# Branch weights ahead of the gate quarters in a group's loads, and the token sums of a layer in 40 GpSimd pieces

## The chip, the cores and the metric

The kernel runs on one core of a Trainium2 chip. The metric is the device time of one execution in microseconds (us), the median of several runs. Engines are named as in the profile: PE is TensorE, DVE is VectorE, ACT is ScalarE, POOL is GpSimd, SP is SyncE, whose queue (SPq) issues most DMAs here.

## The reference, cut to what matters

Two layers of an encoder with 768 tokens (512 of a prompt, 256 of a sample), width 1024. Each layer projects the normed input `h` to three token mixers (A, B, C), to their SiLU gates `z` and to their sigmoid gates `g`, merges the branches and projects once more:

```python
for i, y_i in enumerate((ya, yb, yc)):
    z = cols(COL_Z + i * BRANCH_WIDTH, BRANCH_WIDTH)
    g = cols(COL_G + i * D_MODEL, D_MODEL)
    u = jax.nn.sigmoid(g) * ((y_i * jax.nn.silu(z)) @ w_br[i])
    merged = u if merged is None else merged + u
out = merged @ w_out
return x + gate[:, None, :] * out
```

Everything is fp32. A product of fp32 precision is made of three matmuls on a high and a low part of each operand (`w_hi`, `w_lo`, `act_hi`, `act_lo`): ACT rounds the high part, DVE subtracts it for the low part.

## The kernel before

**Units.** The whole program is one list, `UNITS`. Each engine walks through this list in a loop of its own and does its share of each unit, so the program order on every engine is that of the list, and semaphores tie the engines together. A layer has, in this order: units `("q", l, kind, h, g, t)`, the projection of one tile of 128 tokens to query, key and value of one head (24 matmuls of 128x384 on PE, 6 tiles a head; mixer C has three head groups g), with the attention of earlier tiles between; units `z` for the SiLU gates (8 for each mixer, those of C last); then the gate stage, 12 groups `(l, kind, j)` of 11 units each, kinds in the order C, A, B with four groups each; then 16 output units `o`.

**A group of the gate stage.** The gate projection `h @ w_g` of a group is made by seven products in place of eight (a Strassen-like scheme on halves of the tokens and of the contraction). Units `s0` to `s6` are these products, in the order T1, W11, T2, W22, T3, W21, T4, and units `b0` to `b3` are the four blocks of the branch projection `y @ w_br`. Each of the 11 units is 12 matmuls of 128x384. The four quarters W12, W11, W22, W21 of the group's gate weights are loaded by `load_quarters`, POOL makes T1 to T4 of them (`combos`, 128x512 each), ACT and DVE split each into `s_hi` and `s_lo`. The branch weights are one load of 128x1024 (`load_branch`, into one of two buffers `wb_raw` by turns), split by `branch_high` on ACT (`wb_hi`, line 1718) and `branch_low` on DVE (`wb_lo`, line 2254).

**What runs one group ahead.** While PE works on a group, the others prepare the next one. ACT calls `branch_high` of the next group at unit `s3`, ahead of the sigmoids of `s3` to `s6`. DVE calls `branch_low` of the next group at unit `s4`, ahead of the sums of product T3 (`add_up`, lines 2233 and 2236). PE may start `s6` of the group only when the first of those sums (`U3`) is there. All three engines work strictly in their order.

**Loads of the stage.** `load_groups` on SP calls for each group `load_quarters` (but for the first group of a layer, whose quarters come earlier), then `load_branch`, then, for the first group of A and of B, `load_back`, which brings the parked output `y_t` of that mixer back. The queue waits in its order: W12 of a group for the use of `w12` by the group before (`combo_ready` of T3), W11, W22 and W21 for the group before to finish its units `s1`, `s3` and `s5`, and the branch weights for `b3` of the group two before, whose buffer they take. `back_high` on ACT and `back_low_part` on DVE split `y_t` in the units `s5` to `b0` of these two groups, and their `b0` needs the four results.

**Token sums.** The scheme also needs sums of quadrants of the activations, S1 to S4, in `mix_raw` (128 x 4 x 4 x 384). POOL makes them in `mixes(l)`: ten `tensor_tensor` instructions of 128x1536 one behind the other. They stand at unit `("q", l, "C", 0, 2, 0)` in POOL's program, but wait only for the end of `move_high` and `move_low` (`hi_moved`, `lo_moved`: the activations are put in the order of mixer C at its first unit) and, in layer 1, for the last outputs of layer 0. ACT and DVE split them (`mix_high`, `mix_low`) beside the last `z` units.

## Time and profile before

| | |
|---|---|
| median of 3 runs | 2671.23 us (2670.93 to 2673.95) |
| the profiled execution | 2670.71 us, its span 2667.1 us |
| PE busy | 2376.2 us (89%) |
| DVE busy | 1592.4 us (60%) |
| ACT busy | 1118.9 us (42%) |
| POOL busy | 251.2 us (9%), 219 instructions |
| DMA | mean 70 GB/s |
| mean granted PE clock | 0.948 of full speed |

The span is what the profiler saw between the first and the last instruction; the 3.6 us to the execution's time lie outside of it. A row of a timeline is: start, duration (both in us from the span's start), engine, line, instruction, output and inputs, sizes, count, and in brackets the idle time before it with what ended it. Ends of matmuls are modelled, so the pace of PE is read from starts. A wait is put down to the last of several releasers.

### The profile page before, as it was taken

The page shows a single profiled execution, that of the slowest core. Times are in us where ns is not written, and L with a number is a line of the kernel's source. Part 1 is how long each engine was busy: PE and PEld are TensorE (multiplying, and loading weights), DVE is VectorE, ACT ScalarE, POOL GpSimd, SP SyncE. Part 2 cuts the span into 40 slices and gives each one's busy share as a digit, 9 for nine tenths or more (in the row PEclk, how much of TensorE's full clock was granted, in tenths as well). Part 3 has the DMA queues.
Part 4 walks back from the last instruction along what each step waited for, and adds up shares of the span by engine and source line. Part 5 has one row for each costly group of instructions (what it writes and reads, how often), then busy time and mean ns, then how long its engine had stood idle before and what let it go on. Part 6 is the DMA issues. An engine that isn't in the chain of part 4 may idle for free.

```text
span 2667.1 us, 41810 instructions
## 1 busy us (share of the span) xinstructions
PE 2376.2 (89%) x15466; PEld 2195.4 (82%) x15466; DVE 1592.4 (60%) x4305; ACT 1118.9 (42%) x3035; POOL 251.2 (9%) x219
## 2 busy tenths in 40 slices
PE   7999987999999777777999999599999997777789
PEld 5788876999998777777888889499999977777788
DVE  7875678566765433343578757866667653343452
ACT  5666554344444322222446655444444342222230
POOL 0100133000000111111001002600000001111100
PEclk9999998999999888888999999899999998888899
DMA  7112210211113112121520122002111121121213
GB/s 281 69 64 70 102 56 20 87 53 51 49 64 114 43 47 70 48 69 42 161 70 31 41 94 61 26 27 105 51 53 51 74 83 49 44 76 44 75 58 120
DMA packets 63033, 186.10 MB, mean 70 GB/s; under 512 B 9584, under 2 KB 22512, under 8 KB 59888
## 3 DMA queue, kind: packets, MB, share of 16 engines
q1 hardware_dynamic: 52320, 164.00, 17.8%
q10 hardware_dynamic: 10512, 19.44, 2.1%
q8 instruction: 124, 2.03, 0.3%
q14 instruction: 77, 0.63, 0.1%
HBM read 168.73 MB, written 12.58 MB: 68 GB/s over the span
## 4 chain that ended last, share of the span: by engine, by line
PE 77%; DVE 9%; DMA 5%; ACT 5%; issue 4%; SPq 0%; DVEq 0%; ACTq 0%
PE ps_proj L1034 51%; PE ps_score L1078 7%; PE ps_pt L1078 7%; DMA wb_raw<-in_w_branch 4%; PE ps_score L1211 2%; PE ps_pt L1224 2%; PE ps_pv L1260 1%; PE ps_score L1195 1%; PE ps_tr L1275 1%; PE ps_pv L1241 1%; ACT wb_hi L1718 1%; PE ps_tr L1276 1%; DVE qk L2054 1%; PE ps_pv L1254 1%; DVE w_lo L2316 1%
## 5 line engine op out<-in xcount | busy, mean ns | idle before, releaser
L1034 PE MATMUL ps_proj<-w_hi,act_hi 128*128 128x384 f32 x1824 | 635.3, 348 | 3.3 <-ACT act_hi L1485 2.2
L1034 PE MATMUL ps_proj<-w_lo,act_hi 128*128 128x384 f32 x1824 | 614.1, 337 | 0.0
L1034 PE MATMUL ps_proj<-w_hi,act_lo 128*128 128x384 f32 x1824 | 614.1, 337 | 0.0
L1034 PEld LDWEIGHTS ps_proj<-w_hi,act_hi 128*128 128x128 f32 x1824 | 344.8, 189 | 9.1 <-ACT act_hi L1485 5.8
L1034 PEld LDWEIGHTS ps_proj<-w_lo,act_hi 128*128 128x128 f32 x1824 | 345.2, 189 | 0.0
L1034 PEld LDWEIGHTS ps_proj<-w_hi,act_lo 128*128 128x128 f32 x1824 | 344.3, 189 | 0.0
L2003 DVE TENSOR_REDUCE ssq<-square 128x2 f32<-128x256 f32 (+1 forms) x228 | 95.6, 419 | 251.2 <-ACT square L1579 250.0
L1078 PE MATMUL ps_pt<-act_hi,s_hi 128*128 128x384 f32 x96 | 51.9, 540 | 178.0 <-DVE sum L2233 178.0
L1579 ACT ACTIVATE square<-ps_proj 128x256 f32<-128x256 f32 x228 | 88.1, 386 | 281.5 <-PE ps_proj L1034 281.1
L2316 DVE TENSOR_TENSOR w_lo<-w_raw,w_hi 128x1536 fp32r<-128x1536 f32 (+3 forms) x121 | 188.5, 1559 | 14.5 <-ACT w_hi L1409 13.9
L1034 PE MATMUL ps_proj<-act_hi,w_hi 128*128 128x512 f32 (+1 forms) x512 | 176.1, 344 | 12.7 <-DVE w_lo L2316 9.3
L1409 ACT ACTIVATE w_hi<-w_raw 128x1536 fp32r<-128x1536 f32 (+2 forms) x120 | 161.0, 1342 | 59.7 <-DMA w_raw<-in_w 34.7
L1078 PEld LDWEIGHTS ps_pt<-act_hi,s_hi 128*128 128x128 f32 x96 | 29.6, 308 | 185.0 <-DVE sum L2233 185.0
L1034 PE MATMUL ps_proj<-act_lo,w_hi 128*128 128x512 f32 (+1 forms) x512 | 173.9, 340 | 0.0
L1034 PE MATMUL ps_proj<-act_hi,w_lo 128*128 128x512 f32 (+1 forms) x512 | 173.8, 339 | 0.0
L2254 DVE TENSOR_TENSOR wb_lo<-wb_raw,wb_hi 128x1024 fp32r<-128x1024 f32 x24 | 30.6, 1276 | 218.0 <-ACT wb_hi L1718 218.0
L979 POOL TENSOR_TENSOR s_raw<-w,s_raw 128x512 f32<-128x512 f32 x24 | 32.9, 1370 | 1235.8 <-DMA s_raw<-in_w_gate 1220.5
L1718 ACT ACTIVATE wb_hi<-wb_raw 128x1024 fp32r<-128x1024 f32 x24 | 25.3, 1056 | 286.7 <-DMA wb_raw<-in_w_branch 286.7
L1034 PE MATMUL ps_proj<-yz_hi,wb_hi 128*128 128x384 f32 x384 | 134.5, 350 | 3.1 <-DVE yz_lo L2264 2.8
L1034 PE MATMUL ps_proj<-yz_lo,wb_hi 128*128 128x384 f32 x384 | 132.9, 346 | 0.0
L1034 PE MATMUL ps_proj<-yz_hi,wb_lo 128*128 128x384 f32 x384 | 132.1, 344 | 0.0
L1601 ACT ACTIVATE rstd_ln<-ssq,eps 128x2 f32<-128x2 f32 (+1 forms) x240 | 71.4, 297 | 142.9 <-DVE ssq L2003 142.9
(263 smaller groups left out, 5468.0 us busy)
## 6 DMA issues: line engine op xcount, KB each, us to landing
w_raw<-in_w SPq DMA_DIRECT2D x80, 768.0 KB, 5.1
w_raw<-in_w SPq DMA_DIRECT2D x40, 512.0 KB, 3.8
s_raw<-in_w_gate SPq DMA_DIRECT2D x72, 256.0 KB, 3.3
w_ada<-in_w_mod SPq DMA_DIRECT2D x11, 1536.0 KB, 6.7
wb_raw<-in_w_branch SPq DMA_DIRECT2D x24, 512.0 KB, 4.8
first_ada<-in_w_first SPq DMA_DIRECT2D x8, 1024.0 KB, 12.8
parked<-y_t ACTq DMA_DIRECT2D x4, 1536.0 KB, 6.6
w<-in_w_gate SPq DMA_DIRECT2D x24, 256.0 KB, 4.4
```

The source lines that it names most:

```text
L979: pool.tensor_tensor(s_raw[PLACE[c]][:], first[:], second_[:], ALU.subtract).then_inc(*combo_ready.inc((g, c)))
L1034: op = pe.matmul(out, sta[s](k), mov[m](k), start=(k == 0 and n == 0), stop=(k == chunks - 1 and n == 2))
L1078: op = pe.matmul(sum_bank(u), (s_hi, s_lo)[s][i][:, k, :], moved_in(x, m)[:, k, :], start=opens and k == 0 and n == 0, stop=k == HK - 1 an ...
L1211: op = pe.matmul(ps_score[:, c0:c0 + keys], q, k, start=True, stop=True)
L1224: op = pe.transpose(crossed_probs(a)[:, n * P:(n + 1) * P], probs[ATT_AT[a] % 2][:, c0:c0 + P], ident[:])
L1409: act.activation(w_hi[b][:, c0:n], w_raw[b][:, c0:n], ACT.Copy).then_inc(*w_hi_ready.inc(p))
L1579: act.activation(square[:], made(u, 0, 256), ACT.Square).then_inc(*sq_ready.inc(u))
L1601: act.activation(rstd_ln[:, 0:segs], squares_of(u), ACT.Ln, bias=eps[:], scale=1.0 / d).then_inc(*ln_ready.inc(u))
L1718: act.activation(wb_hi[b][:], wb_raw[b][:], ACT.Copy).then_inc(*wb_hi_ready.inc(g))
L2003: dve.tensor_reduce(squares_of(u), square[:].rearrange("p (s d) -> p s d", s=segs), AX.X, ALU.add).then_inc(*ssq_ready.inc(u))
L2254: dve.tensor_tensor(wb_lo[b][:], wb_raw[b][:], wb_hi[b][:].bitcast(F32), ALU.subtract).then_inc(*wb_lo_ready.inc(g))
L2316: return dve.tensor_tensor(w_lo[b][:, c0:c1], w_raw[b][:, c0:c1], w_hi[b][:, c0:c1].bitcast(F32), ALU.subtract)
```

## The change

In `load_groups` the branch weights of a group are issued ahead of its four quarters:

```diff
             def load_groups(l):
                 for g in groups_of(l):
+                    load_branch(g)
                     if group_before(g):
                         load_quarters(g)
-                    load_branch(g)
                     if g[2] == 0 and g[1] in PARKED:
                         load_back(l, g[1])
```

`mixes(l)` becomes `mix_piece(l, n, k)`, one quarter (128x384) of one of the ten steps. The 40 pieces of a layer stand at 40 successive `q` units of mixer C, beginning with `("q", l, "C", 0, 2, 0)`, and each waits for PE to have finished the projection of its unit:

```diff
+MIX_PIECES = [(n, k) for n in range(10) for k in range(HK)]
...
+            def mix_piece(l, n, k):
...
+                if n > 0:
+                    pool.wait_ge(*mix_step.at((l, n - 1, k)))
+                elif k == 0:
+                    pool.wait_ge(*hi_moved.at((l, KC)))
+                    pool.wait_ge(*lo_moved.at((l, KC)))
...
+                pool.tensor_tensor(out, a, b, op).then_inc(*mix_step.inc((l, n, k)))
...
-                if u[0] == "q" and u[2:] == ("C", 0, 2, 0):
-                    mixes(u[1])
+                if u[0] == "q" and u[2] == "C" and AT[u] >= AT[("q", u[1], "C", 0, 2, 0)]:
+                    at = AT[u] - AT[("q", u[1], "C", 0, 2, 0)]
+                    if at < len(MIX_PIECES):
+                        pool.wait_ge(*proj_ready.at(u))
+                        mix_piece(u[1], *MIX_PIECES[at])
...
-                act.wait_ge(*mix_step.at((l, 9)))
+                act.wait_ge(*mix_step.at((l, *MIX_PIECES[-1])))
```

The number of instructions on PE, DVE, ACT and SP stays the same; POOL has 60 more. Line numbers of the changed kernel are one higher from here on.

SP's queue at the start of the gate stage of layer 0, before (`w` is W12, `s_raw_147`, `_149` and `_151` are W11, W22 and W21, `wb_raw_158` and `_159` the two branch buffers; the first row is the branch load of the layer's first group):

```order
L869 DMA wb_raw_158<-in_w_branch 128x1024 [waits proj_ready]
L860 DMA w_153<-in_w_gate 128x512 [waits combo_ready]
L860 DMA s_raw_147<-in_w_gate 128x512 [waits proj_ready]
L860 DMA s_raw_149<-in_w_gate 128x512 [waits proj_ready]
L860 DMA s_raw_151<-in_w_gate 128x512 [waits proj_ready]
L869 DMA wb_raw_159<-in_w_branch 128x1024 [waits proj_ready]
L860 DMA w_153<-in_w_gate 128x512 [waits combo_ready]
```

The same place in the changed kernel:

```order
L870 DMA wb_raw_158<-in_w_branch 128x1024 [waits proj_ready]
L870 DMA wb_raw_159<-in_w_branch 128x1024 [waits proj_ready]
L861 DMA w_153<-in_w_gate 128x512 [waits combo_ready]
L861 DMA s_raw_147<-in_w_gate 128x512 [waits proj_ready]
L861 DMA s_raw_149<-in_w_gate 128x512 [waits proj_ready]
L861 DMA s_raw_151<-in_w_gate 128x512 [waits proj_ready]
L870 DMA wb_raw_158<-in_w_branch 128x1024 [waits proj_ready]
```

The second group's branch load has moved ahead of the four quarters, and with it ahead of the queue's waits for `s1`, `s3` and `s5` of the first group.

SP's queue where kind A opens in layer 0, in the changed kernel (the parked `y_t` of A, then the next group's loads):

```order
L861 DMA s_raw_151<-in_w_gate 128x512 [waits proj_ready]
L877 DMA y_t<-parked 128x1536 [waits park_done,proj_ready]
L877 DMA y_t<-parked 128x1536
L870 DMA wb_raw_159<-in_w_branch 128x1024 [waits proj_ready]
L861 DMA w_153<-in_w_gate 128x512 [waits combo_ready]
```

The branch load of the group behind now follows the two loads of `y_t` directly, where four quarters stood between before.

POOL's program at the sums of a layer, before (ten instructions, then the first group's combination T1):

```order
L965 TENSOR_TENSOR bias_97<-rel_s,mask_b_sb 128x256 [waits masked]
L965 TENSOR_TENSOR bias_97<-rel_s,mask_b_sb 128x256
L1015 TENSOR_TENSOR mix_raw<-act_hi 128x1536 [waits lo_moved,hi_moved]
L1015 TENSOR_TENSOR mix_raw<-act_lo 128x1536 [waits mix_step]
L1015 TENSOR_TENSOR mix_raw<-mix_raw 128x1536 [waits mix_step]
L1015 TENSOR_TENSOR mix_raw<-act_hi 128x1536 [waits mix_step]
```

The same place in the changed kernel:

```order
L966 TENSOR_TENSOR bias_97<-rel_s,mask_b_sb 128x256 [waits masked]
L966 TENSOR_TENSOR bias_97<-rel_s,mask_b_sb 128x256
L1016 TENSOR_TENSOR mix_raw<-act_hi 128x384 [waits lo_moved,hi_moved,proj_ready]
L1016 TENSOR_TENSOR mix_raw<-act_hi 128x384 [waits proj_ready] x3
L1016 TENSOR_TENSOR mix_raw<-act_lo 128x384 [waits mix_step,proj_ready] x4
L1016 TENSOR_TENSOR mix_raw<-mix_raw 128x384 [waits mix_step,proj_ready] x4
L1016 TENSOR_TENSOR mix_raw<-act_hi 128x384 [waits mix_step,proj_ready] x4
```

Each instruction of before is four now, and each of them waits for a projection unit of its own (`proj_ready`).

## Rows read from the trace of the kernel before

**Rows 1.** The page: the span, and the chain that ended last, by line.

```profile
span 2667.1 us, 41810 instructions
...
PE ps_proj L1034 51%; PE ps_score L1078 7%; PE ps_pt L1078 7%; DMA wb_raw<-in_w_branch 4%; PE ps_score L1211 2%; PE ps_pt L1224 2%; PE ps_pv L1260 1%; PE ps_score L1195 1%; PE ps_tr L1275 1%; PE ps_pv L1241 1%; ACT wb_hi L1718 1%; PE ps_tr L1276 1%; DVE qk L2054 1%; PE ps_pv L1254 1%; DVE w_lo L2316 1%
```

**Rows 2.** Waits of the whole span: us in total, times, longest.

```profile
ACT wb_hi L1718 <- DMA wb_raw<-in_w_branch: 286.7, 22, 13.7
...
PE ps_pt L1078 <- DVE sum L2233: 178.0, 22, 8.9
```

**Rows 3.** Timeline of one group of kind C, layer 0, engine by engine.

```profile
960.76 8.65 SPq L860 DMA_DIRECT2D s_raw<-in_w_gate  x3
969.46 0.43 SPq L869 DMA_DIRECT2D wb_raw<-in_w_branch  x1
...
974.25 1.06 ACT L1718 ACTIVATE wb_hi<-wb_raw 128x1024 fp32r<-128x1024 f32 x1 [12.99 <-DMA wb_raw<-in_w_branch]
...
975.34 1.23 DVE L2254 TENSOR_TENSOR wb_lo<-wb_raw,wb_hi 128x1024 fp32r<-128x1024 f32 x1 [9.86 <-ACT wb_hi L1718]
...
977.09 0.69 PE L1078 MATMUL ps_pt<-act_hi,s_hi 128*128 128x384 f32 x1 [8.04 <-DVE sum L2233]
...
983.95 0.33 PE L1034 MATMUL ps_proj<-yz_hi,wb_hi 128*128 128x384 f32 x1
...
990.19 0.33 PE L1078 MATMUL ps_score<-mix_hi,s_hi 128*128 128x384 f32 x1
```

**Rows 4.** The chain in order of time: first and last branch wait of layer 0.

```profile
902.16 5.67 DMA wb_raw<-in_w_branch
...
1240.07 4.65 DMA wb_raw<-in_w_branch
```

**Rows 5.** Parked `y_t`: landing times of its DMAs; the opening of kind A.

```profile
DMA to landing us min/median/max: 4.3/5.9/7.6
...
1046.72 1.83 DVE L2264 TENSOR_TENSOR yz_lo<-y_t,yz_hi 128x768 fp32r<-128x768 f32 x2 [1.32 <-ACT yz_hi L1731]
...
1051.30 0.44 PE L1034 MATMUL ps_proj<-yz_hi,wb_hi 128*128 128x384 f32 x1 [0.32 <-DVE yz_lo L2264]
```

**Rows 6.** Windows: us, busy time of PE, PEld, DVE, ACT, POOL, granted clock, DMA.

```profile
388.80:424.50 35.70, 8.28 (x52) 7.42 (x51) 35.29 (x24) 4.17 (x16) 34.58 (x11) 0.69 0.02 4
1698.00:1734.00 36.00, 9.17 (x56) 8.07 (x52) 35.62 (x23) 4.54 (x18) 34.95 (x11) 0.66 0.02 4
...
914.00:1260.00 346.00, 263.86 (x1370) 259.20 (x1370) 131.08 (x213) 83.97 (x154) 52.01 (x41) 0.86 0.16 54
...
425.00:870.00 445.00, 442.48 (x3418) 415.71 (x3418) 288.74 (x1033) 196.93 (x564) 5.08 (x4) 0.99 0.19 66
```

**Rows 7.** The start of mixer C, layer 0: the sums on POOL, DVE, PE.

```profile
L1015 POOL TENSOR_TENSOR mix_raw<-act_hi x4: 3416/3418/3428, 388.8 to 1709.0; 128x1536 f32<-128x1536 f32 x4
...
396.14 6.81 DVE L2118 TENSOR_SCALAR probs<-probs,rden 128x256 f32<-128x256 f32 x2
402.86 0.41 DVE L2003 TENSOR_REDUCE ssq<-square 128x2 f32<-128x256 f32 x1
...
390.01 0.66 PE L1224 MATMUL ps_pt<-ident,probs 128*128 128x128 f32 x4
403.00 1.11 PE L1224 MATMUL ps_pt<-ident,probs 128*128 128x128 f32 x4 [12.33 <-DVE probs L2118]
...
424.51 0.45 PE L1275 MATMUL ps_tr<-ident,qk 128*128 128x128 f32 x1 [15.10 <-DVE qk L2054]
...
431.47 0.70 PE L1211 MATMUL ps_score<-qkv 64*128 64x256 f32 x4
```

**Rows 8.** A combination on POOL (page), and a later unit's end in mixer C.

```profile
L979 POOL TENSOR_TENSOR s_raw<-w,s_raw 128x512 f32<-128x512 f32 x24 | 32.9, 1370 | 1235.8 <-DMA s_raw<-in_w_gate 1220.5
...
612.02 0.39 ACT L1579 ACTIVATE square<-ps_proj 128x256 f32<-128x256 f32 x1 [2.74 <-PE ps_proj L1034]
...
613.22 0.42 DVE L2017 TENSOR_TENSOR turned<-gained,rope_c_sb 128x256 f32<-128x256 f32 x1
```

More of the change, by code:

```diff
@@ L648, in build @@
         gated = tally("gated", [(g, m) for g in ALL_GROUPS for m in BLOCKS])
-        mix_step = tally("mix_step", [(l, n) for l in layers for n in range(10)])
+        mix_step = tally("mix_step", [(l, *p) for l in layers for p in MIX_PIECES])
         mix_hi_ready = tally("mix_hi_ready", [(l, m) for l in layers for m in MIXES])
@@ L995, in combos @@
                 combine("T4", s_raw[PLACE["W21"]], s_raw[PLACE["T2"]])
-            def mixes(l):
-                hi = {x: quadrant(act_hi, x).bitcast(F32) for x in ("11", "12", "21", "22")}
-                lo = {x: quadrant(act_lo, x).bitcast(F32) for x in ("11", "12", "21", "22")}
-                s1, s2, s3, s4 = (mix_raw[:, i] for i in range(4))
-                pool.wait_ge(*hi_moved.at((l, KC)))
-                pool.wait_ge(*lo_moved.at((l, KC)))
-                if l > 0:
-                    for p in range(2 * KC - 3, 2 * KC):
-                        pool.wait_ge(*y_kept[p % 3].at((l - 1, p)))
-                todo = ((s1, hi["21"], hi["22"], ALU.add), (s2, lo["21"], lo["22"], ALU.add), (s1, s1, s2, ALU.add),
-                        (s3, hi["11"], hi["21"], ALU.subtract), (s4, lo["11"], lo["21"], ALU.subtract), (s3, s3, s4, ALU.add),
-                        (s2, s1, hi["11"], ALU.subtract), (s2, s2, lo["11"], ALU.subtract),
-                        (s4, hi["12"], s2, ALU.subtract), (s4, s4, lo["12"], ALU.add))
-                for n, (out, a, b, op) in enumerate(todo):
-                    if n > 0:
-                        pool.wait_ge(*mix_step.at((l, n - 1)))
-                    pool.tensor_tensor(out, a, b, op).then_inc(*mix_step.inc((l, n)))
@@ new lines, in mix_piece @@
+            def mix_piece(l, n, k):
+                hi = {x: quadrant(act_hi, x).bitcast(F32)[:, k, :] for x in ("11", "12", "21", "22")}
+                lo = {x: quadrant(act_lo, x).bitcast(F32)[:, k, :] for x in ("11", "12", "21", "22")}
+                s1, s2, s3, s4 = (mix_raw[:, i, k, :] for i in range(4))
+                out, a, b, op = ((s1, hi["21"], hi["22"], ALU.add), (s2, lo["21"], lo["22"], ALU.add), (s1, s1, s2, ALU.add),
+                                 (s3, hi["11"], hi["21"], ALU.subtract), (s4, lo["11"], lo["21"], ALU.subtract),
+                                 (s3, s3, s4, ALU.add), (s2, s1, hi["11"], ALU.subtract), (s2, s2, lo["11"], ALU.subtract),
+                                 (s4, hi["12"], s2, ALU.subtract), (s4, s4, lo["12"], ALU.add))[n]
+                if n > 0:
[3 more added lines that the diff above has]
+                    pool.wait_ge(*lo_moved.at((l, KC)))
+                    if l > 0:
+                        for p in range(2 * KC - 3, 2 * KC):
+                            pool.wait_ge(*y_kept[p % 3].at((l - 1, p)))
+                pool.tensor_tensor(out, a, b, op).then_inc(*mix_step.inc((l, n, k)))
```

## The prediction, made before the change was timed

> **What bounds the kernel now.** I read the page first. PE is busy for 89% of the span and the chain that ended last is mostly its matmuls, but 4% of that chain is the landing of one kind of DMA, the branch weights `wb_raw`, with their split on ACT behind it [rows 1]. 4% of 2667 us is over 100 us on the critical path, for a load whose data nobody needs at that moment. The list of waits gives the length of the queue behind it: ACT stood for 286.7 us before `wb_hi`, 22 times, and PE for 178.0 us, 22 times, before `ps_pt`, released by the DVE sum of line 2233 [rows 2]. 22 is 11 of the 12 groups in each of two layers: all groups that have a group behind them.
>
> The timeline of one group shows how these are one chain [rows 3]. SP's queue issues three quarters of the next group from 960.76 on, each after a unit of the present group, and only when the last has been released by the end of `s5` does the branch load follow, at 969.46. It lands 4.8 us later, ACT splits it (974.25, 1.06 us), DVE makes the low part (975.34, 1.23 us), and only then comes to the sum that `s6` needs. PE starts `s6` at 977.09 after 8.04 us of idling. So `s6` of each group waits for the branch weights of the next one, for no reason of data: ACT and DVE stand in their program order at a load that is issued after `s5`.
>
> Then I looked for stretches where PE is idle elsewhere. In mixer C PE is busy for 442.5 of 445 us at a clock of 0.99; there nothing is to be had. But in the 35.7 us before, PE is busy for 8.3 us while POOL and DVE are both full; it is the same in layer 1 [rows 6]. There POOL makes the token sums. DVE instructions that take a fraction of a microsecond elsewhere stretch there: two scalings of 256 columns take 6.81 us, two lengths of a POOL instruction of 3.42 us. Others do not: a reduction in the middle of it takes 0.41 us [rows 7]. So DVE instructions of some kinds wait for the running POOL instruction, one after the other, and PE waits for them, 12.33 us for `probs` and 15.10 us for `qk` [rows 7].
>
> **Part 1, the branch load ahead of the quarters.** In the new order the load of the next group is issued when `b3` of the group before the present one is done, that is, when the present group starts, as the buffer is free from there. Everything it was behind (the waits for `s1`, `s3`, `s5`) is now behind it. It lands about 5 us into the group, by 4.8 us of flight [rows 3]; a unit is 12 matmuls, and at the pace between 983.95 and 990.19 (36 starts in 6.24 us, 0.173 each) 2.08 us long [rows 3]. ACT comes to `branch_high` when it has kept the product of `s1`, 4.7 us in, and stands there for half a microsecond at most; DVE comes to `branch_low` after the sum of `s3`, 8.9 us in, and finds its data. The sum behind it needs `s4` and is made at 10.4 to 11 us, ahead of the start of `s6` at 12.5 us.
>
> What it is worth: the 8.09 us of idling (178.0 / 22), and what the clock takes behind it. From 977.09 to 990.19 there are 60 matmuls in 13.10 us, where the full pace takes 10.40: 2.70 us more [rows 3]. Together 10.8 us a group. The chain confirms it: the branch waits of layer 0 lie 33.8 us apart (337.9 us for ten) [rows 4], 132 matmuls at full pace are 22.9 us, difference 10.9. 22 x 10.8 = **237 us**.
>
> What is late next in a group? The queue's moved neighbours: W12 of the next group was issued behind the branch load at `s5` and is now issued behind it at the start of the group, 12.5 us before it would matter, as T1 needs W11 too, which still waits for `s1`. W11, W22 and W21 still wait for the same units, so T2 and T3 (POOL, 1.3 to 1.4 us each [rows 8]) are ready 14.6 us in, T4 at about 17.5 us, and their splits before the group's end at 22.9 us. T2 is needed by `s2` of the next group, 4 us beyond. DVE is busy for 131 us and ACT for 84 us in the 346 us of ten groups [rows 6], 13 and 8 us of the 22.9. I find no new wait in an ordinary group, and 0 is my value for it. PE then runs without a gap; the stretch of 445 us with such work had a clock of 0.99 [rows 6], so I take the full one.
>
> The exception is the opening group of A and B, four in all. The two loads of `y_t` (0.77 MB each) are issued at the start of the group, landing within 7.6 us [rows 5], and the 0.5 MB of branch weights now fly right behind them. By that pace they land about 10 us in: `branch_high` ends at 11, `branch_low` at 12.3, the sum at 12.9, so `s6` starts half a microsecond late. Then `back_high` on ACT starts behind the sigmoid of the second sum, at about 14 us, and its four parts with the work between end near 18, while `b0` would want them from 14.6 us on. In the trace of before this chain already leaves 0.32 us of wait at `b0`, with an `s6` that ran at the low clock [rows 5]; with a fast one 2 us of cover are gone. I take 2.5 us for each (0 to 5.5, the upper end with a low clock again), **10 us** in all. The Trainium skill, "SBUF — State Buffer", section "The DMA setup-cost knee", fits a transfer as 2 us plus its bytes at 436 GB/s. By an estimate from that page the three loads (2.1 MB) would have landed after 6.8 us and the sum would be some 4 us lower; the trace has 7.6 us for the first two alone, so I stay with it.
>
> **Part 2, the sums in pieces.** Removed is the block of ten POOL instructions at the start of mixer C. In layer 0 PE had sent four transposes at 390.01 and the next scores at 431.47. Between them lie four transposes, two pairs for `qk` and 48 matmuls: 0.66 + 2 x 0.33 + 8.3 = 9.6 us [rows 7]. DVE, which needs 289 us for 442 us of PE's work in mixer C [rows 6], is not behind PE when nothing holds it. So the scores come at about 400.3 instead of 431.5: 31 us. Layer 1 had an idle time of 26.8 us against 27.4 [rows 6]: 30.5 us. Together **61.5 us**.
>
> Added are 40 pieces a layer in the stretch where PE has no slack. Their length isn't in the trace; bounds are the nearest rows: 3.42 us for 1536 columns and 1.3 us for 512 [rows 7, 8], which by a straight line gives about 1.0 us for 384. A piece starts when its unit's projection is done. At that moment DVE waits for ACT's square: in the row, ACT starts the square at 612.02, and the first DVE instruction of a kind that had waited for POOL (`turned`) starts at 613.22 [rows 8]. Between them stand only the reduction and the product from PSUM. A piece from 611.95 to 613.0 fits. Where the split of a weight piece still runs on DVE (two in six units), the piece starts up to 0.6 us later and `turned` is pushed by that. PE takes the result two units on, with some 2 us in hand. Cost on the path: from 0 (all covered) to 80 x 1.0 us (each one on the path); I take 2 us, as nearly all of it is covered.
>
> **Sum.** Profiled execution 2670.7 (0.5 us under the median) - 237 + 10 - 61.5 + 2 = 2384 us.
>
> **Rivals.** (a) *A new wait in the groups.* Something of the group's preparation is late at the full pace (DVE's low parts held up by POOL's combinations, or the branch weights landing after 9 us in all groups): 2 us of wait and 2.7 us of low clock in 22 groups give back 103 us, 2487 us. Against it: the slack of 1.5 us at `s6` and 4 us at T2; for it: DVE and POOL instructions can hold each other up [rows 7]. Chance 0.08.
>
> (b) *The pieces land on DVE's path.* If every DVE instruction that meets a piece waited, or the pieces started late, half of the 80 would cost 1 us: 2424 us, at most 2464. For it: in this stretch PE is released by DVE's `qk` in each unit. Against it: the reduction at 402.86 ran at its length beside POOL. Chance 0.08.
>
> (c) *The idle time at the start of mixer C has another cause* (the reordering of the activations, the moves of values), and stays: 2445 us. Against it: two lengths of POOL's instruction in one row. That the branch load doesn't start earlier is excluded by the order of the queue. Chance 0.02.
>
> (d) *Slower.* The pieces cost a fixed time and not one by columns: 3.4 us each, as the whole instruction, and each holds DVE up. 80 x 3.4 = 272 us on the path, 2654 us; it passes the time of before from 3.6 us a piece on. The combination of 512 columns at 1.4 us [rows 8] speaks against it. Chance 0.01.
>
> **The numbers.** The forecast has 0.81. Its own bounds are 2370 (openings free, pieces free) and 2412 (openings at 5.5 us each, pieces at 10 us, 10 us of small waits in the groups); I put the range to 2370 to 2415, which leaves out (a), most of (b), (c) and (d), some 0.2. 0.2% of this time is 5 us, about what a measurement can tell from no change. Faster 0.98, the same 0.01, slower 0.01.
>
> **What the new profile would show.** Right: no `wb_hi` wait of over 1 us but in openings; `ps_pt <- sum L2234` gone from PE's waits; branch loads 22.9 to 23.5 us apart, openings 25 to 26; PE over 97% busy in the gate stage at a clock near 1; POOL's 80 pieces at 1.0 us each; mixer C starting with no PE wait over 1 us, and staying 445 us long. Wrong: PE waiting at `s2`, `s6` or `b0` in ordinary groups (rival a), or waits of PE for `qk` or `probs` through mixer C with DVE rows of 1 us and more (rival b).

## The result, and the profile after the change

The changed kernel takes **2392.2 us** (median of 4 runs, 2391.6 to 2394.9) against 2671.1 us for the kernel before (4 runs, 2670.8 to 2674.0): 0.8956 of its time, with a 95% interval of 0.894 to 0.8971. The prediction was 2384 us with a range of 2370 to 2415.

The page of the changed kernel, as [rows 1]. Line numbers are one higher than before on SP's and POOL's side (lines 861 to 1016), and four higher from 1038 on, for PE, ACT and DVE:

```profile
span 2389.9 us, 41943 instructions
PE 2326.4 (97%) x15466; PEld 2152.0 (90%) x15466; DVE 1540.0 (64%) x4305; ACT 1120.8 (47%) x3035; POOL 283.9 (12%) x279
...
PE ps_proj L1038 57%; PE ps_score L1082 8%; PE ps_pt L1082 6%; PE ps_score L1215 2%; PE ps_pt L1228 2%; PE ps_pv L1264 2%; PE ps_score L1199 1%; PE ps_tr L1279 1%; PE ps_pv L1245 1%; PE ps_tr L1280 1%; PE ps_pv L1258 1%; DVE w_lo L2320 1%; DMA w_raw<-in_w 1%; DVE top L2078 1%; ACT act_hi L1489 1%
```

The 4% of `wb_raw` have left the chain, and PE is busy for 97% of the span. The list of waits of the changed kernel (us in total, times, longest), as [rows 2]:

```profile
ACT wb_hi L1722 <- DMA wb_raw<-in_w_branch: 11.7, 4, 3.1
PE ps_proj L1038 <- DVE yz_lo L2268: 11.0, 8, 2.2
```

ACT's wait for the branch weights went from 286.7 us in 22 places to 11.7 us in 4, all in openings. PE's wait for the sum ahead of `s6` (178.0 us) is gone from the list. What is there now is a wait of PE for `yz_lo`, the low halves of the returning `y_t`, in the same four openings. It was there before as well, but shorter (0.32 us in A and 1.13 us in B of layer 0).

The timeline of an ordinary group of kind C in the changed kernel, as [rows 3] (start, duration, and in brackets the idle time before):

```profile
980.37 0.33 SPq L870 DMA_DIRECT2D wb_raw<-in_w_branch  x1
...
1003.25 0.33 SPq L870 DMA_DIRECT2D wb_raw<-in_w_branch  x1
...
984.92 1.05 ACT L1722 ACTIVATE wb_hi<-wb_raw 128x1024 fp32r<-128x1024 f32 x1
989.17 1.22 DVE L2258 TENSOR_TENSOR wb_lo<-wb_raw,wb_hi 128x1024 fp32r<-128x1024 f32 x1
991.37 0.56 DVE L2240 TENSOR_TENSOR sum<-sum,kept 128x384 f32<-128x384 f32 x1
```

The branch load goes out at the group's start, ACT splits it 4.55 us in without a wait, DVE 8.8 us in, and the next group begins 22.88 us behind this one: 132 matmuls at 0.173 us. Every group that follows an ordinary group is 22.88 us behind it, within 0.01 us.

The windows of the changed kernel, as [rows 6] (us, busy time of PE, PEld, DVE, ACT and POOL, granted clock, DMA share, GB/s):

```profile
388.80:424.50 35.70, 35.69 (x254) 33.16 (x254) 30.47 (x124) 22.92 (x80) 0.78 (x2) 1.00 0.11 38
425.00:797.00 372.00, 372.00 (x2861) 354.89 (x2858) 245.14 (x876) 157.37 (x456) 44.09 (x40) 1.00 0.17 61
```

At the start of mixer C, PE was busy for 8.3 of 35.7 us and is now busy for all of it. In the stretch that holds the 40 pieces of POOL, PE is busy without a gap, at a granted clock of 1.00.

**Where the time went**, by marks that stand at the same work in both traces:

| stretch | before | after | difference |
|---|---|---|---|
| first scores behind the idle time, layer 0 | 431.5 us | 400.6 us | -30.9 |
| last weight load of mixer C, layer 0 | 828.7 us | 797.8 us | -30.9 |
| first branch load of the gate stage, layer 0 | 886.7 us | 857.3 us | -29.4 |
| length of the gate stage, layer 0, from there to the same mark in the output units | 403.8 us | 296.7 us | -107.1 |
| length of the gate stage, layer 1, same marks | 403.5 us | 295.7 us | -107.8 |

The two gate stages gave 214.9 us; the forecast had 237 - 10 = 227. The start of mixer C gave 30.9 us in each layer (in layer 1 the last weight load of mixer C stands 167.4 us earlier, of which 136.6 had been gained by the mark at the end of layer 0), 61.8 together; the forecast had 61.5. That makes 276.7 of the 277.2 us of span. Between the first two marks nothing is lost to the 40 pieces. The third mark moves by itself: in the seven later kernels that are the same up to there (those of the last two parts below) it stands between 854.3 and 859.3 us. So the miss lies in the gate stages, and there mostly in the openings. From the issue of `y_t` to the next branch load an opening takes 27.54, 29.19, 28.07 and 29.16 us, where 22.88 would do: 22.4 us in all and not 10.

Another 1.5 us is the first group of layer 0, and shows that the clock behind a short wait is not the same each time. PE waits 2.28 us in the first group of both layers, before the change and after it. These are its two rows in the changed kernel:

```profile
865.80 0.66 PE L1082 MATMUL ps_score<-act_hi,s_hi 128*128 128x384 f32 x1 [2.28 <-issue]
...
2037.70 0.41 PE L1082 MATMUL ps_score<-act_hi,s_hi 128*128 128x384 f32 x1 [2.28 <-issue]
```

Behind the first, PE starts eight matmuls 0.32 us apart before it is back at 0.173; behind the second it is at full pace at once. The third branch load follows the first by 26.88 us in layer 0 and by 25.41 in layer 1.

### The profile page after: what moved, and what is told of

It reads as the page before. It is cut to its first block, busy times and chain, and to the rows that moved or that the text cites. A ratio compares the mean times of both kernels' runs of the same rounds, so it can differ in the third digit from the quotient of the medians.

```text
span 2389.9 us, 41943 instructions
## 1 busy us (share of the span) xinstructions
PE 2326.4 (97%) x15466; PEld 2152.0 (90%) x15466; DVE 1540.0 (64%) x4305; ACT 1120.8 (47%) x3035; POOL 283.9 (12%) x279
## 4 chain that ended last, share of the span: by engine, by line
PE 86%; DVE 6%; ACT 4%; issue 2%; DMA 1%; SPq 0%; DVEq 0%; ACTq 0%
PE ps_proj L1038 57%; PE ps_score L1082 8%; PE ps_pt L1082 6%; PE ps_score L1215 2%; PE ps_pt L1228 2%; PE ps_pv L1264 2%; PE ps_score L1199 1%; PE ps_tr L1279 1%; PE ps_pv L1245 1%; PE ps_tr L1280 1%; PE ps_pv L1258 1%; DVE w_lo L2320 1%; DMA w_raw<-in_w 1%; DVE top L2078 1%; ACT act_hi L1489 1%
## 5 line engine op out<-in xcount | busy, mean ns | idle before, releaser
L2252 DVE TENSOR_TENSOR s_lo<-s_raw,s_hi 128x512 fp32r<-128x512 f32 x168 | 116.8, 719 | 23.6 <-ACT s_hi L1717 23.6
L1038 PEld LDWEIGHTS ps_proj<-act_hi,w_hi 128*128 128x128 f32 x512 | 98.5, 192 | 25.6 <-issue 10.3
L960 POOL TENSOR_TENSOR bias<-rel_p,mask_b_sb 128x128 f32<-128x128 f32 x64 | 31.7, 528 | 711.9 <-DVE top L2086 409.4
L1689 ACT ACTIVATE kept<-ps_score 128x384 f32<-128x384 f32 x48 | 23.4, 491 | 191.1 <-PE ps_score L1082 191.1
## 6 DMA issues: line engine op xcount, KB each, us to landing
first_ada<-in_w_first SPq DMA_DIRECT2D x8, 1024.0 KB, 12.4
```

The lines of the kernel that those rows point to most:

```text
L1038: op = pe.matmul(out, sta[s](k), mov[m](k), start=(k == 0 and n == 0), stop=(k == chunks - 1 and n == 2))
L2252: dve.tensor_tensor(s_lo[i][:], s_raw[i][:], s_hi[i][:].bitcast(F32), ALU.subtract).then_inc(*s_lo_ready.inc((g, c)))
```

## The experiments

All kernels here compute the full result. Ratios are to the kernel before on the same chip. Differences in us are to the 2392.2 us of the changed kernel (ratio 0.8956), where nothing else is said; the kernel before took between 2667.5 and 2672.5 us beside these runs, so such a difference holds to some 3 or 4 us.

### Do the two parts act apart?

The first run takes the new order of the loads alone, with the ten whole instructions left as they were:

```diff
                 for g in groups_of(l):
+                    load_branch(g)
                     if group_before(g):
                         load_quarters(g)
-                    load_branch(g)
```

> Kernel before with the new order of the loads alone; the token sums stay one block of ten instructions ahead of mixer C. Theory 1, the two parts act in different stretches and add: the 22 waits of ScalarE for the branch weights go with the low clock behind them (22 times 10.8 us = 237 us), the four openings of kinds A and B give back 22 us, as in the changed kernel, so 2671 - 237 + 22 = 2456 us; TensorE still waits 12.3 + 15.1 us at the start of mixer C of each layer. Theory 2, the wait at the start of mixer C was not caused by the block of sums: the load order alone gives all of it, and the time is the changed kernel's 2392 us.

Measured: 2454.1 us (2454.0 to 2457.1), ratio 0.9199. The second run is the changed kernel with this edit undone, so that only the pieces are new.

> Changed kernel with the old order of the loads: only the 40 pieces are new. Theory 1, the parts add: 2671 - 62 (twice 31 us at the start of mixer C) = 2609 us, and ScalarE waits 22 times for the branch weights as before. Theory 2, the pieces do nothing for the path (the 31 us come from elsewhere): 2671 us. If the pieces cost time in the 78 units of mixer C, it shows as more than 2609.

Measured: 2606.9 us (2604.8 to 2611.9), ratio 0.9766. Before took 2667.5 us beside these two, so the parts are worth 213.4 and 60.7 us alone, 274 together, and the changed kernel's ratio makes 278.5 of the same 2667.5. They add up within the spread of the runs, and the order of the loads has nothing to do with the start of mixer C. In the run with the pieces alone ACT's wait for the branch weights is back in full, 285.2 us in 22 places.

### What made the start of mixer C expensive?

The block of ten whole instructions again, with the new order of the loads, but one projection unit inside mixer C:

```diff
+                if u[0] == "q" and u[2:] == ("C", 0, 2, 0):
+                    pool.wait_ge(*proj_ready.at(u))
+                    mixes(u[1])
```

> New order of the loads, and the token sums as ten instructions over whole tiles in one block again, but behind the first projection unit of mixer C and not ahead of it. Theory 1, what costs is that VectorE's operations cannot run beside a block of GpSimd instructions of 3.4 us each, wherever it stands: the 27 us of idle TensorE move one unit on and shrink by no more than a few us, 2392 + 2 x 25 = 2442 us (2425 to 2456). Theory 2, what costs is the place ahead of mixer C, where the scores and the first unit wait for something else: then this kernel takes 2392 us.

Measured: 2451.9 us (2450.9 to 2452.8), ratio 0.9188, the same as with the block at its old place (2454.1). The block costs 60 us at either place. Its timeline on DVE shows how:

```profile
486.48 0.42 DVE L2010 TENSOR_TENSOR gained<-ps_proj,row 128x256 f32<-128x256 f32 x1
486.94 2.63 DVE L2018 TENSOR_TENSOR turned<-gained,rope_c_sb 128x256 f32<-128x256 f32 x1
489.49 3.67 DVE L2021 TENSOR_TENSOR crossed<-gained,rope_c_sb 128x256 f32<-128x256 f32 x1
493.08 3.37 DVE L2031 SCALAR_TENSOR_TENSOR newton<-ssq,rstd 128x2 f32<-128x2 f32 x1
...
496.58 3.37 DVE L2040 TENSOR_TENSOR newton<-newton,rstd 128x2 f32<-128x2 f32 x1
...
503.57 3.63 DVE L2055 TENSOR_TENSOR qk<-turned,newton 128x256 f32<-128x256 f32 x1
507.12 5.01 DVE L2317 TENSOR_TENSOR w_lo<-w_raw,w_hi 128x1536 fp32r<-128x1536 f32 x1
512.05 0.41 DVE L2004 TENSOR_REDUCE ssq<-square 128x2 f32<-128x256 f32 x1
...
522.74 0.15 DVE L2040 TENSOR_TENSOR newton<-newton,rstd 128x2 f32<-128x2 f32 x1
```

An instruction on two values per partition takes 3.37 us where it takes 0.15 us once the block is over (522.74): it waits for a whole POOL instruction, and the next POOL instruction slips in ahead of the next DVE one. Six such rows up to `qk` (one more `newton` is left out) make the 16.4 us that PE waits for it here; two more left out, of 0.28 us, got through, each in the 0.1 us between two POOL instructions. Not all kinds wait: the product that reads PSUM (`gained`, 0.42 us) and the reduction of one operand (0.41 us) run beside POOL at their own length. POOL's instructions end at 489.28, 492.87, 496.43, 499.92, 503.42 and 506.92, each at most 0.3 us ahead of the end of a DVE row that waits. The Trainium skill, "SBUF — State Buffer", section "🔬 SBUF: two separate sides", states that VectorE and GpSimd share one pair of ports as an exclusive lock, which a GpSimd instruction takes, or a VectorE instruction with two operands in SBUF (or one in a two-port mode), whichever starts first, and holds for the whole instruction. The trace agrees by kind: instructions with two operands in SBUF wait (3.37 us for 0.15), the one with an operand in PSUM does not (0.42 us).

Next, the same ten whole instructions, one behind each of the first ten units:

```diff
-MIX_PIECES = [(n, k) for n in range(10) for k in range(HK)]
+MIX_PIECES = [(n, 0) for n in range(10)]
```

> Changed kernel, but the same token sums as ten instructions over whole tiles (3.4 us each), one behind each of the first ten projection units of mixer C, in place of 40 pieces (1.0 us each). If spreading is what counts, VectorE's slack in a unit of 4.97 us takes 3.4 us too and the time is 2392 us. If the length of one instruction counts, a VectorE operation that TensorE waits for stands up to 3.4 us behind it: up to 20 x 2.4 = 48 us more and a low clock behind some of them, 2410 to 2440 us. I take 2405.

Measured: 2408.7 us (2408.1 to 2412.1), ratio 0.9028, 16.5 us over the changed kernel. The row of a window over the ten instructions of layer 0 in this kernel:

```profile
480.00:560.00 80.00, 73.75 (x620) 69.57 (x619) 69.52 (x173) 31.64 (x91) 36.00 (x10) 0.98 0.15 54
```

and of the same window in the changed kernel:

```profile
480.00:560.00 80.00, 80.00 (x670) 76.62 (x668) 51.92 (x194) 34.62 (x102) 15.13 (x14) 1.00 0.20 73
```

Spreading the work gives three quarters of the gain (60 to 16.5 us), its shorter pieces the rest. Whole instructions stand before a DVE step of nearly every one of these units, and at four places of layer 0 this is more than PE has in hand. The rows of the first of them on DVE and PE:

```profile
488.52 2.63 DVE L2021 TENSOR_TENSOR turned<-gained,rope_c_sb 128x256 f32<-128x256 f32 x1
...
491.73 3.39 DVE L2043 TENSOR_TENSOR newton<-newton,rstd 128x2 f32<-128x2 f32 x1
...
496.10 0.30 PE L1279 MATMUL ps_tr<-ident,qk 128*128 128x128 f32 x1 [3.62 <-DVE qk L2058]
```

The other half of the question is short pieces in a row, ahead of mixer C:

```diff
-                if u[0] == "q" and u[2] == "C" and AT[u] >= AT[("q", u[1], "C", 0, 2, 0)]:
...
+                if u[0] == "q" and u[2:] == ("C", 0, 2, 0):
+                    for piece in MIX_PIECES:
+                        mix_piece(u[1], *piece)
```

> Changed kernel, but its 40 pieces stand in one block at the place of the old ten instructions, ahead of mixer C, with no wait for TensorE between them. GpSimd's work is then 40 x 1.02 = 41 us a layer in one stretch. Theory 1, a VectorE operation cannot start until the GpSimd instruction under way has ended: each of VectorE's operations that TensorE waits for there loses up to 1.0 and not up to 3.5 us, so that 27.4 us of TensorE's waiting a layer become about 8, and with the low clock behind it the time is 2392 + 2 x (8 to 15) = 2408 to 2422 us. Theory 2, what counts is GpSimd's busy time as a whole, whatever its pieces: 2392 + 60 = 2452 us. Theory 3, only the place counts, pieces are free there too: 2392 us.

Measured: 2432.5 us (2429.6 to 2433.6), ratio 0.91: 40 us over the changed kernel, two thirds of the whole block's 60. No theory had this number; the first, nearest with 2408 to 2422, has the mechanism and counted too little. Its timeline on DVE:

```profile
394.83 1.22 DVE L2022 TENSOR_TENSOR crossed<-gained,rope_c_sb 128x256 f32<-128x256 f32 x1
...
396.93 1.11 DVE L2039 TENSOR_TENSOR turned<-turned,crossed 128x128 f32<-128x128 f32 x1
397.96 0.97 DVE L2041 TENSOR_TENSOR newton<-newton,rstd 128x2 f32<-128x2 f32 x1
...
399.06 0.97 DVE L2046 SCALAR_TENSOR_TENSOR newton<-newton,rstd 128x2 f32<-128x2 f32 x1
400.16 1.09 DVE L2056 TENSOR_TENSOR qk<-turned,newton 128x256 f32<-128x256 f32 x1
...
401.36 1.92 DVE L2120 TENSOR_SCALAR probs<-probs,rden 128x256 f32<-128x256 f32 x2
```

Five instructions lose 0.7 to 0.8 us each against their lengths elsewhere (0.42, 0.28, 0.15, 0.15, 0.43) and the two scalings about 1 us together: some 5 us per unit. The pieces last for 43 us and DVE takes 9.5 us a unit there, so that 4.5 units lose 5 us each, 22 us a layer. The measured 20 us a layer are close to that. My estimate had scaled PE's waits by the length of a piece, and left out that four times as many pieces can catch four times as many instructions.

### How late may the branch load be?

In the next two runs the load is issued behind W11 and behind W22 of the quarters:

```diff
                     sp.dma_start(dst[:], w_gate[n, :, at]).then_inc(*quarter_in[q].inc(g))
+                    if branch and q == "W11":
+                        load_branch(g)
```

> Changed kernel, but in the groups that have quarters to fetch the branch load is issued behind the first quarter (W11) and not ahead of it, so 0.5 MB more stands before it and it starts one step of TensorE later. Theory 1, there is a threshold: with the issue at the group's start the load lands some 7 to 8 us in and is wanted some 14 us in, so behind W11 it still lands before ScalarE asks, the splitting never waits, and the time is 2392 us within 3 us. Theory 2, every us of delay costs: 22 waits grow by the 2.6 us of a step, 2392 + 57 = 2449 us.

Measured: 2400.7 us (2398.3 to 2404.3), ratio 0.898. ACT waits in all 22 groups now, but ordinary groups stay 22.88 us apart (a few 23.0 to 23.3, in layer 1 above all). Its waits, and its row on ACT in an ordinary group (issued at 1009.72):

```profile
ACT wb_hi L1725 <- DMA wb_raw<-in_w_branch: 100.5, 22, 5.9
...
1014.30 1.06 ACT L1725 ACTIVATE wb_hi<-wb_raw 128x1024 fp32r<-128x1024 f32 x1 [4.46 <-DMA wb_raw<-in_w_branch]
```

So 4.5 us of waiting on ACT cost nothing there: there is a threshold. The next run shows that the group has little more in hand: there ACT waits 8.7 us a group and PE 3.85, which leaves 4.9. The 8.5 us more are the openings, where the load flies behind `y_t` and is now issued 4.5 us later still: they take 30.8, 30.6, 30.9 and 30.5 us (between branch loads, which stand at the same place of each group here), 8.7 us more in all than in the changed kernel. Here PE does wait for the sum ahead of `s6`, 0.66 to 0.97 us, as the prediction had it for the changed kernel, and then three times for `yz_lo`: 4.0 us an opening where it was 2.7. The rest is low clock. Neither theory had put a cost there. (The ratio's interval, 0.8967 to 0.8993, just touches that of the changed kernel; it is the traces that place the difference.)

> As the run behind W11, but the branch load is issued behind the third quarter (W22), one quarter short of the order of the kernel before. In the kernel before ScalarE waited until 13.5 us into the group for the weights and TensorE stood for 8.0 us. One quarter earlier is one step earlier: the load lands some 2.6 to 4 us sooner, TensorE stands for 4 to 5.5 us and the clock still falls behind it. 22 x (4 to 5.5 + 2.7) = 147 to 180 us above 2392, so 2540 to 2570 us. If instead TensorE's wait does not move with the load, it is nearer 2629.

Measured: 2508.9 us (one run, no interval), 116.7 over the changed kernel, below the 147 to 180 I had expected. Its waits:

```profile
ACT wb_hi L1725 <- DMA wb_raw<-in_w_branch: 191.6, 22, 9.2
...
PE ps_pt L1085 <- DVE sum L2240: 84.7, 22, 4.2
```

PE waits 3.85 us a group, against 8.09 before: one quarter earlier is worth 4.2 us, the distance of two units. Its ordinary groups are 28.4 to 29.7 us apart, 6.2 over 22.88 on average, so that some 2.3 us a group are low clock. By the starts of PE behind the wait (35 of them, against 0.173 us each) the low clock took 1.5 to 2.9 us, 2.2 on average of 18 groups, and in the kernel before 1.4 to 2.9 us, 2.3 on average, behind a wait twice as long. The shorter wait did not buy a shorter stretch of low clock. The whole is 116.7 us and not 22 x 6.2 = 136, as the openings take 30.6 us here, 2.1 more than in the changed kernel: 18 x 6.2 + 4 x 2.1 = 120.

### What do the openings wait for?

The prediction said: for the branch weights, which land late behind `y_t`. Against this stands the order of VectorE's own work. Timeline of the changed kernel where kind B opens in layer 0 (first rows SP's queue, then ACT, DVE, POOL and PE):

```profile
1049.01 0.80 SPq L877 DMA_DIRECT2D y_t<-parked  x2
1049.86 0.43 SPq L870 DMA_DIRECT2D wb_raw<-in_w_branch  x1
...
1056.57 1.06 ACT L1722 ACTIVATE wb_hi<-wb_raw 128x1024 fp32r<-128x1024 f32 x1 [2.90 <-DMA wb_raw<-in_w_branch]
...
1061.05 1.56 ACT L1735 ACTIVATE yz_hi<-y_t 128x768 fp32r<-128x768 f32 x2
...
1059.42 0.56 DVE L2237 TENSOR_TENSOR sum<-ps_pt,kept 128x384 f32<-128x384 f32 x1 [0.39 <-PE ps_pt L1082]
1061.92 2.89 DVE L2268 TENSOR_TENSOR yz_lo<-y_t,yz_hi 128x768 fp32r<-128x768 f32 x2 [1.33 <-ACT yz_hi L1735]
1064.73 1.76 DVE L2252 TENSOR_TENSOR s_lo<-s_raw,s_hi 128x512 fp32r<-128x512 f32 x1
...
1066.88 1.81 DVE L2268 TENSOR_TENSOR yz_lo<-y_t,yz_hi 128x768 fp32r<-128x768 f32 x2
...
1064.56 1.38 POOL L980 TENSOR_TENSOR s_raw<-s_raw,s_raw 128x512 f32<-128x512 f32 x1 [1.44 <-DMA s_raw<-in_w_gate]
...
1064.08 0.41 PE L1038 MATMUL ps_proj<-yz_hi,wb_hi 128*128 128x384 f32 x1 [0.54 <-DVE yz_lo L2268]
1067.88 0.69 PE L1038 MATMUL ps_proj<-yz_hi,wb_hi 128*128 128x384 f32 x1 [2.23 <-DVE yz_lo L2268]
```

The branch weights have landed by 1056.57, 7.6 us into the group, and the sum for `s6` is held up by PE's own `s4` and not by them. PE stands 0.54 and 2.23 us at the first unit of the way back (`b0`), for the two pairs of `yz_lo`, and the second pair is made behind `s_lo`, which takes 1.76 us beside POOL's T4 (1064.56) where it takes 0.69. The rest of the price is the clock: from 1067.88 to 1073.81 PE starts 18 matmuls 0.33 us apart, 2.8 us more than at full pace. The windows show it as granted clock:

```profile
1063.00:1070.00 7.00, 4.22 (x17) 3.24 (x16) 5.69 (x6) 5.51 (x11) 1.50 (x2) 0.79 0.06 23
1070.00:1077.00 7.00, 7.00 (x32) 7.00 (x31) 4.81 (x9) 0.11 (x1) 0.00 (x0) 0.73 0.00 0
```

Five runs tell the theories apart. The first loads the branch weights ahead of `y_t`:

```diff
-                    load_branch(g)
+                    opens = g[2] == 0 and g[1] in PARKED
+                    if not (g[2] == 1 and g[1] in PARKED):
+                        load_branch(g)
...
+                    if opens:
+                        load_branch(group_after(g))
                         load_back(l, g[1])
```

> Changed kernel, but at the four openings of kinds A and B the branch load of the following group is issued ahead of y_t and not behind it. Each opening lasts 4.7 to 6.3 us longer than an ordinary group (22 us in all). Theory 1 (the prediction's: the branch weights land late behind y_t and the chain behind them slips): the openings shrink by most of that, 2392 - 15 = 2377 us (2370 to 2382). Theory 2 (it is the order of VectorE's work before the first unit of the way back: the recombination of y_t and four operations that take turns with GpSimd's combinations): nothing changes, 2392 within 2 us.

Measured: 2393.1 us (2388.8 to 2395.0), ratio 0.8953: no change. ACT's wait for the branch weights is gone from all openings (no such row is left in its list), and PE stands exactly as long as before:

```profile
1060.76 0.41 PE L1041 MATMUL ps_proj<-yz_hi,wb_hi 128*128 128x384 f32 x1 [0.54 <-DVE yz_lo L2271]
1064.56 0.69 PE L1041 MATMUL ps_proj<-yz_hi,wb_hi 128*128 128x384 f32 x1 [2.23 <-DVE yz_lo L2271]
```

Over all four, the openings are 20.1 us over ordinary groups and not 22.4. Of these 2.3 us only 0.7 are less waiting (10.3 us in all against 11.0), the rest is clock. So the prediction's reason, the late landing, is not what they wait for. The second run puts the recombination of `y_t` one unit earlier on ACT and DVE:

```diff
-                    if g[1] in PARKED and g[2] == 0 and at in (5, 6):
-                        for k in (2 * at - 10, 2 * at - 9):
+                    if g[1] in PARKED and g[2] == 0 and at in (4, 5):
+                        for k in (2 * at - 8, 2 * at - 7):
...
-                    if g[1] in PARKED and g[2] == 0 and at in (6, 7):
-                        for k in (2 * at - 12, 2 * at - 11):
+                    if g[1] in PARKED and g[2] == 0 and at in (5, 6):
+                        for k in (2 * at - 10, 2 * at - 9):
```

> Changed kernel, but in the four openings ScalarE's and VectorE's recombination of y_t for the way back stands one unit earlier in their orders, so that TensorE's first unit of the way back finds its operands. Theory 2 (VectorE's order before that unit makes the cost): most of the 22 us of the openings goes, their wait of 0.5 + 2.2 us and the low clock behind it, 2392 - 16 = 2376 us (2370 to 2382). Theory 1 (late landing of the branch weights): y_t lands too late as well and the operations only wait where they now stand, 2392 within 3 us or a little more, up to 2396.

Measured: 2385.1 us (2381.6 to 2387.0), ratio 0.8919; less than half of what I expected. On DVE the four low halves are now in one row, and on POOL two combinations beside them:

```profile
1056.51 6.86 DVE L2268 TENSOR_TENSOR yz_lo<-y_t,yz_hi 128x768 fp32r<-128x768 f32 x4
...
1057.72 2.00 POOL L980 TENSOR_TENSOR s_raw<-s_raw,w 128x512 f32<-128x512 f32 x1
1060.56 1.99 POOL L980 TENSOR_TENSOR s_raw<-s_raw,s_raw 128x512 f32<-128x512 f32 x1 [0.84 <-DMA s_raw<-in_w_gate]
```

Four low halves take 3.6 us alone (1.81 for two above), a combination 1.29. Here both engines are longer than alone, DVE by 3.2 us and each combination by 0.7 us. So the third run moves T4 out of the way:

```diff
                 pool.wait_ge(*combo_ready.at((g, "T2")))
+                if before and before[2] == 0 and before[1] in PARKED:
+                    pool.wait_ge(*proj_ready.at(("b", *before, 0)))
                 combine("T4",
```

> Changed kernel, but in the group behind an opening GpSimd's last combination (T4) waits for the first unit of the way back, so that it does not run beside VectorE's low halves of y_t. If GpSimd's combinations are a part of what holds VectorE there, s_lo takes 0.69 and not 1.76 us, the second pair of low halves is ready 1.1 us sooner, and each opening is 1.1 to 2 us shorter: 2392 - 6 = 2386 us (2384 to 2388). If TensorE waits for the order of VectorE's work alone: 2392 us.

Measured: 2381.6 us (2379.7 to 2384.1), ratio 0.8912. The openings are 6.9 us shorter in all, near the expected 6, but only 2.4 us of them are less waiting of PE (8.6 us for 11.0). The rest is clock: in the two openings of layer 1 it stayed at 1.00, behind waits of 0.79 + 1.15 and 1.50 + 1.15 us. The rest of the difference is not the edit's: the first branch load stands at 854.7 us and not at 857.3, where the kernels are the same, and the first group is without the 1.5 us of low clock. `s_lo` is back at its own length, as expected:

```profile
1060.59 0.68 DVE L2254 TENSOR_TENSOR s_lo<-s_raw,s_hi 128x512 fp32r<-128x512 f32 x1
```

The fourth run has both edits.

> The recombination of y_t one unit earlier and GpSimd's T4 behind the first unit of the way back, together. With the former alone 6.5 of the 22 us of the openings went (2385 us), and VectorE's four low halves of y_t still took 6.86 us in a row, where 3.6 would do without GpSimd beside them. If GpSimd holds VectorE there, T4's 2 us are gone from that stretch and each opening gets 1.5 us shorter, 2385 - 6 = 2379 us. If not, 2385 us.

Measured: **2374.3 us** (2371.5 to 2377.8, 5 runs), ratio 0.8883 with an interval of 0.887 to 0.8895, which lies clear of the changed kernel's: 0.7% faster than it. PE's only listed wait in the opening of B, and the window around it:

```profile
1057.64 0.41 PE L1040 MATMUL ps_proj<-yz_hi,wb_hi 128*128 128x384 f32 x1 [0.89 <-DVE yz_lo L2270]
...
1056.00:1063.00 7.00, 5.93 (x30) 4.69 (x29) 6.97 (x9) 4.76 (x10) 1.97 (x2) 1.00 0.08 29
```

One wait of 0.89 us remains of 0.54 and 2.23, and the granted clock stays at 1.00, as it does in the other three openings (waits of 0.80, 0.93 and 1.10 us). The four low halves take 4.66 us in a row now and not 6.86, with one combination beside them and not two. The four openings take 24.65, 25.00, 24.43 and 25.27 us, 7.8 over ordinary groups and not 22.4. These 14.6 us are most of the 17.9 between the medians; another 2.4 lie ahead of the gate stage (854.9 against 857.3) and 1.5 in its first group, where the kernels are the same. The fifth run adds the branch load ahead of `y_t`.

> The two edits of the run before and the branch load of the following group ahead of y_t. The load order alone shortened the openings by 2 us in all; once VectorE's order is out of the way, the landing of the branch weights (ScalarE waited 2.8 to 4.2 us for them in the openings) is what stands next in ScalarE's order ahead of the recombination. If so, this kernel beats the one with two edits by 1 us an opening: 2375 us. If the landing plays no part, it equals it: 2379 us. If y_t, now issued behind 2 MB more, lands too late for its earlier place, it is slower than that: up to 2384 us.

Measured: 2377.0 us (2374.4 to 2379.3), ratio 0.8894 (0.8881 to 0.8906). Inconclusive: its openings sum to 6.3 us over ordinary groups, 1.6 less than with two edits, but its profiled execution reached the first branch load at 859.3 us and not at 854.9, with the same program up to there, and the ranges overlap. An effect of 1.6 us is below what these runs can tell.

## Why the prediction was right, and where it was not

**The 22 waits.** 22 x 10.8 = 237 us was right in mechanism and size. The branch loads before stood 33.8 us apart on average, 10.9 over 22.88; 22 times that is 239 us, and less the 22.4 of the openings and the 1.5 of the first group it makes the 214.9 that the gate stages gave, within 0.3. The price of the clock was read from one group (2.70 us) and happened to be near the upper end of its range (1.4 to 2.9 us in ordinary groups); the spacing of the chain, 10.9, was the better ground. The split by one unit after another came as worked out: ACT 4.55 us in (said 4.7), DVE 8.8 (said 8.9), the second sum at 11.0 (said 10.4 to 11). No new wait took its place in ordinary groups (rival a).

**The openings: the mis-sized term.** Predicted 4 x 2.5 us, measured 4 x 5.6, a little over the upper end of 5.5 that it had given. The failed step is "`branch_high` ends at 11 ... so `s6` starts half a microsecond late". The branch weights landed 7.6 us in and not 10, `branch_high` ended 8.6 us in, and nothing waited for them; with the load ahead of `y_t` the waits of PE in the opening of B were the same. The next step, `back_high` ending near 18 as the thing that `b0` waits for, was not it either: it began 12.0 us in (said 14) and ended 16.0 us in. What PE waited for were the low parts on DVE, whose length the prediction had not worked out: the last pair starts 17.9 us in, behind `s_lo`, and PE goes on at 18.9. Left out were POOL's combinations beside `yz_lo` and `s_lo`, which rival (a) had named for ordinary groups only, and the low clock, which I put into the upper bound of 5.5 us and not into the value. In the opening of B the two waits are 2.8 us of its 6.3; the other 3.5 are mostly the clock, 2.8 us of it behind the second wait. With T4 out of the way and the order one unit earlier 14.6 of the 22.4 us go.

The three loads of an opening are where I preferred my own estimate of 10 us to that of the Trainium skill, "SBUF — State Buffer", section "The DMA setup-cost knee": 6.8 us for the three. The trace shows the last one usable 7.6 us after the first issue, so the skill's figure was the nearer. The 4 us less that its figure would have given the sum did not come either, as the openings never hung on that landing.

**The start of mixer C.** Predicted 31 us in layer 0, measured 30.9; the scores stand at 400.56 (said 400.3). The cause is shown: the block costs 60 us at either place, and a DVE instruction of a kind that waits loses one POOL instruction. Rival (c) fell.

**The pieces.** Predicted 2 us, measured 0 in the profile: 1.016 us a piece at the median and 1.10 on average (estimated 1.0 by a straight line), PE busy for 372.00 of 372 us beside them. Rivals (b) and (d) fell. That whole instructions at the same places cost 16.5 us shows that this was not given: there DVE instructions that meet a POOL instruction do land on PE's path, as rival (b) had it.

**Sum.** 2670.7 - 214.9 (gate stages) - 61.8 (starts of mixer C) - 0.5 (elsewhere) is 2393.5; 1.7 us less lie outside the span than before, which makes 2391.8, the profiled execution's own time. Against 2384 the terms are +12.4 for the openings and +1.5 for the first group, -2 for the pieces and -2 for the 22 waits, and 2.5 us less of everything else. The range held with room in it: its upper end (by its own terms 2414) had some 18 us for the pieces and for small waits in the groups that were not needed, and the openings alone used up theirs.

## What to carry to other kernels

A load belongs in its queue ahead of waits that its own buffer doesn't need, and its deadline is where the first engine in program order meets it, not where the data is used: up to that point (here 4.5 us behind the moment when ACT comes to it) lateness is free, behind it every microsecond of PE's waiting is paid, and here 1.4 to 2.9 us of low clock on top, for a wait of 3.85 us as for one of 8.1. Work put on GpSimd is paid for by VectorE, by the instruction: many short ones at moments when VectorE waits for something else cost nothing, the same ones in a row cost two thirds of the long block. When a chain is cut, look for the place where it had covered something else, follow every engine's share there to the end, and count with low clock behind what wait remains.

## What the runs showed of the hardware that I had not expected

- Even a DVE instruction on two values per partition (0.15 us alone) takes 3.37 us beside POOL instructions of 3.4 us, and several in a row lose nearly a full POOL instruction each: the starts of the two engines alternate, instruction by instruction.
- POOL is held up by DVE as well. Of the four 128x512 combinations of an ordinary group three take 1.29 us, and T3, which DVE's `s_lo` meets, 1.76; beside the `yz_lo` row one took 2.00 us.
- Forty POOL instructions of 1.02 us in a row cost the kernel two thirds of what ten of 3.42 us do (40 us against 60), although each blocks for less than a third of the time.
- The low clock behind a wait of PE did not follow the length of the wait: 2.3 us on average behind 8.1 us (kernel before), 2.2 behind 3.85 us (load behind W22), 1.4 to 2.9 in both.
- Behind short waits it could come or not. The same 2.28 us was followed by low clock in layer 0 of the changed kernel and not in layer 1; with T4 later 0.87 + 1.15 us was, and 1.50 + 1.15 us was not. Behind the single waits of 0.80 to 1.10 us of the run with both edits the clock stayed at 1.00. So a microsecond or two between two kernels can be this alone.
